# Modulation slots of the mlp_out stage: two ahead of each of its four output products, in place of four behind each of the first two

## The chip, the cores and the metric

The kernel runs on one core of a Trainium2 chip. The metric is the device time of one execution in microseconds (us). Shown with it are the span that the profiler records on that core and the TensorE clock that was granted, as a share of full speed.

## The reference, cut to what matters

The reference is a small transformer over 512 tokens of width 1024: a gMLP layer with its feed-forward part, an attention layer with its own, then a second block. A conditioning vector `c` gives each layer its shifts, scales and gates:

```
c_act = silu(c)
mod = c_act @ ada_w[layer] + ada_b[layer]            # 1024 x 6144, for two layers
sh_m, sc_m, g_m, sh_f, sc_f, g_f = split(mod, 6)
h = modulate(rms_norm(x, pre_mix_g), sh_m, sc_m)
y = gmlp_mixer(h, ...)                               # ends in (u * mixed v) @ w_out: 512x2048 @ 2048x1024
x = x + g_m * rms_norm(y, post_mix_g)
...
k, v, dcum = shared_kv(x, c_act @ kv_ada_w + kv_ada_b, ...)   # 1024 x 2048
```

The product `@ w_out` is the stage `mlp_out`. Beside it the kernel works on the products of `c_act` with the big modulation matrices. In this stage those are the two 1024-column halves of `kv_ada_w`, which are not needed before the layer behind the feed-forward part.

## The kernel before, in words

**Products.** Each matrix product is a stage of groups of 256 output columns. A group of `mlp_out` has four units of weights; a unit is four chunks of 128 rows by 256 columns (512 KB). There are four groups, called 0 to 3 here, in the code (i, j) = (0, 0), (0, 1), (1, 0), (1, 1). A unit goes through a ring of four buffers: SyncE (SP) loads `raw` (L358), ScalarE (ACT) makes `w_hi` (L702), GpSimd (POOL) makes `w_lo` in place of `raw` (L708), and TensorE (PE) takes 12 products of 256 columns for each chunk, three for each of four blocks of tokens (L1254). A buffer's next load waits on `w_used` until PE is through with the unit in it. So the first unit of a group can be loaded once the first unit of the group before has been used.

**Group 0** runs beside the token mixing: PE makes a mixed chunk (L1412), VectorE (DVE) forms `tmp` from it (L1817, L1823), ACT and POOL split it into `y_hi` and `y_lo` (L876, L1165), four chunks ahead of their use. After its last `tmp`, DVE runs `gain_copy(0)` (L1703).

**Epilogue of a group.** ACT splits all four units of the next group, then takes square sums of the finished one (L860). DVE multiplies the finished sums by a gain into `y_mlp` (`product_group`, L1725). That frees the accumulator for the group after the next.

**Modulation slots.** A slot is two chunks of 128 rows by 1024 columns of a modulation matrix (512 KB each). Slot s has the chunks 2s and 2s + 1. SP loads a chunk into one of two buffers (`ada_load`, L419) and waits before that on `ada_used`, until DVE has used the chunk two before it. DVE multiplies and adds it into `ada_wide` (`ada_chunk`, L1630 for the first chunk of eight, L1633 for the others). After four slots (eight chunks) `ada_wide` is complete; PE sums it over partitions in `wide_columns(q)` (L1305, 8 small products), and only when DVE has read that result (`wide_finish(q)`, L1646) does it start the next eight chunks. `wide_finish(q)` is called by DVE at the first chunk of the next four slots. Slots 12 to 15 make q = 3, slots 16 to 19 make q = 4, slots 20 to 23 make q = 5.

**The order on the queues in mlp_out.** SP carries its instructions out strictly in the order written: an instruction that waits holds up all loads behind it. In the kernel before it loads the eight units of groups 0 and 1; then slot 16, unit 0 of group 2, slot 17, unit 1, slot 18, unit 2, slot 19, unit 3, and in the same way slots 20 to 23 with the units of group 3. DVE runs slots 16 to 19 after the product of group 0, and slots 20 to 23 after the product of group 1. PE calls `wide_columns(3)` ahead of chunk 8 of group 0, and `wide_columns(4)` ahead of chunk 2 of group 2. `wide_columns(5)` comes with the next stage, `gu0`.

The waits behind this order are these (the first two at L418 and L356):

```
sp.wait_ge(ada_used, n + 1)     # ada_load of chunk n; ada_used starts at 2
sp.wait_ge(w_used, n + 1)       # load_unit of unit n; w_used starts at RING = 4
pe.wait_ge(ada_ready, ADA_SETUP - ADA_PAIRS + q + 1)      # wide_columns(q)
dve.wait_ge(ada_sum, ADA_SETUP - ADA_PAIRS + q + 1)       # wide_finish(q)
```

Of the kernel before, what the change touches and what calls it, by code (L numbers as in the profile page):

```python
# [120 lines left out]
def build_program(nc, io):  # L121
    S = number_stages()
    ctx = ExitStack()
    with ctx:
# [220 lines left out]
        def unit_no(st, i, j, x):  # L345
            return st.unit0 + i * st.per_body + (len(st.units[0]) if j else 0) + x

        def slot_of(st, i, j, x):

            n = unit_no(st, i if isinstance(i, int) else 0, j, x)  # L350
            return n % RING


        def load_unit(sp, st, src, i, j, x):
            n, s, (k0, nk) = unit_no(st, i, j, x), slot_of(st, i, j, x), st.units[j][x]
            sp.wait_ge(w_used, n + 1)  # L356
            for dst, ap in src(i, j, k0, nk, raw[:, s, 0:nk, :]):
                sp.dma_start(dst, ap).then_inc(landed[s], 16)  # L358
# [7 lines left out]
        src_of = {}  # L366
# [47 lines left out]
        def ada_load(sp, n):  # L414

            wide, k = 2 + n // DC, n % DC
            w, c0 = (ada_w[0], wide) if wide < 6 else (kv_ada_w, wide - 6) if wide < 8 else (ada_w[1], wide - 8)
            sp.wait_ge(ada_used, n + 1)  # L418
            sp.dma_start(ada_raw[:, n % 2, :], w[k * P:(k + 1) * P, ADA_WIDE * c0:ADA_WIDE * (c0 + 1)]).then_inc(ada_landed[n % 2], 16)  # L419

        def ada_slot_load(sp, slot):
            ada_load(sp, 2 * slot)
            ada_load(sp, 2 * slot + 1)

        def load_group(sp, name, i, j):
            st = S[name]
            for x in range(len(st.units[j])):
                load_unit(sp, st, src_of[name], i, j, x)

        def load_stage(sp, name, ada=None, unroll=False, skip=0):  # L430

            st = S[name]
            def group(i, j):
                load_group(sp, name, i, j)
                if ada:
                    ada(i, j)
            def body(i):
                group(i, 0)
                group(i, 1)
            if skip % 2:  # L440
                group(skip // 2, 1)
            first = (skip + 1) // 2
            if unroll or st.iters - first <= 1 or st.per_body % RING:

                for i in range(first, st.iters):
                    body(i)
            else:
                with sp.Fori(first, st.iters) as i:
                    body(i)
# [248 lines left out]
        def split_hi(act, st, i, j, units=slice(None)):  # L698
            for x, (_, nk) in list(enumerate(st.units[j]))[units]:
                s = slot_of(st, i, j, x)  # L700
                act.wait_ge(landed[s], landed_value(st, i, j, x))
                act.activation(w_hi[:, s, 0:nk, :], raw[:, s, 0:nk, :], ACT.Copy).then_inc(w_split_hi, 1)  # L702

        def split_lo(eng, st, i, j, units=slice(None)):
            for x, (_, nk) in list(enumerate(st.units[j]))[units]:
                s = slot_of(st, i, j, x)
                eng.wait_ge(w_split_hi, unit_no(st, i, j, x) + 1)
                eng.tensor_tensor(w_lo[:, s, 0:nk, :], raw[:, s, 0:nk, :], w_hi[:, s, 0:nk, :].bitcast(F32),  # L708
                                  ALU.subtract).then_inc(w_split, 1)
# [7 lines left out]
        def sums_tok(j):  # L717
            return acc[:, j].rearrange("p a (b n) -> p (a b) n", b=2)
# [3 lines left out]
        def _(sp):  # L722
# [31 lines left out]
            ada_slot_load(sp, 1)  # L754
            load_stage(sp, "mlp_u", lambda i, j: ada_slot_load(sp, 2 * i + j), skip=2, unroll=True)
            load_stage(sp, "mlp_v", lambda i, j: ada_slot_load(sp, 8 + 2 * i + j), unroll=True)
            load_group(sp, "mlp_out", 0, 0)
            load_group(sp, "mlp_out", 0, 1)
            st = S["mlp_out"]
            for j in range(2):  # L760
                for x in range(len(st.units[j])):
                    ada_slot_load(sp, 16 + len(st.units[0]) * j + x)
                    load_unit(sp, st, src_of["mlp_out"], 1, j, x)
            load_stage(sp, "gu0", lambda i, j: ada_slot_load(sp, 24 + 2 * i + j), unroll=True)
            load_group(sp, "down0", 0, 0)
            ada_slot_load(sp, 46)
# [481 lines left out]
        def _(pe):  # L1248
# [51 lines left out]
            def wide_columns(q):  # L1300

                pe.wait_ge(ada_ready, ADA_SETUP - ADA_PAIRS + q + 1)
                pe.wait_ge(ada_col, ADA_SETUP - ADA_PAIRS + q)
                for m in range(ADA_WIDE // P):
                    ins = pe.matmul(ada_ps[:, m:m + 1], ada_wide[:, m * P:(m + 1) * P], ones[:, 0:1], start=True, stop=True)  # L1305
                ins.then_inc(ada_sum, 1)
# [97 lines left out]
            def mix_tokens(g):  # L1404

                if g % V_PART == 0:
                    pe.wait_ge(v_norm, NB // 2 * (g // V_PART + 1))
                    pe.wait_ge(v_norm_act, NB // 2 * (g // V_PART + 1))
                if g >= 2:
                    pe.wait_ge(mix_read, g - 1)  # L1410
                for b in range(NB):
                    ins = pe.matmul(aux[:, g % 2, b * P:(b + 1) * P], v[:, b, g * P:(g + 1) * P], ws_t[:, g, :], start=True, stop=True)  # L1412
                ins.then_inc(mix_ps, 1)

            def mixing_beside(i, j, k):

                if (i, j) == (0, 0) and k + AHEAD < GC:
                    mix_tokens(k + AHEAD)
                if (i, j, k) == (0, 1, 0):
                    pe.wait_ge(gain_ready, 1)  # L1420
                if (i, j, k) in ((0, 0, 8), (1, 0, 2)):
                    wide_columns(3 + i)
            for g in range(AHEAD):
                mix_tokens(g)
# [194 lines left out]
        def _(dve):  # L1619
# [3 lines left out]
            def ada_chunk(n):  # L1623

                q, k = divmod(n, DC)
                if k == 0 and q:
                    wide_finish(q - 1)
                dve.wait_ge(ada_landed[n % 2], 16 * (n // 2 + 1))
                if k == 0:
                    dve.tensor_scalar(ada_wide[:], ada_raw[:, n % 2, :], c_act[:, 0:1], None, ALU.mult).then_inc(ada_used, 1)  # L1630
                else:
                    dve.drain()
                    dve.scalar_tensor_tensor(ada_wide[:], ada_raw[:, n % 2, :], c_act[:, k:k + 1], ada_wide[:], ALU.mult, ALU.add) \  # L1633
                        .then_inc(ada_used, 1)
                if k == DC - 1:
                    dve.drain().then_inc(ada_ready, 1)

            def ada_slot(slot):
                ada_chunk(2 * slot)
                ada_chunk(2 * slot + 1)  # L1640
# [31 lines left out]
            def modulation(gain, scale):  # L1672

                dve.scalar_tensor_tensor(scol[:], scale, 1.0, gain, ALU.add, ALU.mult)
                dve.drain()
# [25 lines left out]
            def gain_copy(n):  # L1701
                dve.wait_ge(gain_ps, n + 1)
                dve.tensor_copy(gain_row[:].rearrange("p (a t) -> p a t", a=2), sums(1)).then_inc(gain_ready, 1)  # L1703
                dve.drain()

            def add_square_sums(n, g):

                dve.wait_ge(sq_ready, 8 * n + 2 * g + 2)
                if g:
                    ins = dve.tensor_tensor(square_sum[:, 4, :], square_sum[:, 0 if g == 1 else 4, :], square_sum[:, g, :], ALU.add)  # L1710
                    if g == 3:
                        ins.then_inc(sum_ready, 1)
                    else:
                        dve.drain()

            def product_group(n, g, y):

                cols = slice(g * COLS, (g + 1) * COLS)
                for half in range(2):
                    blocks = slice(2 * half, 2 * half + 2)  # L1720
                    if half:
                        add_square_sums(n, g)
                    else:
                        dve.wait_ge(sq_ready, 8 * n + 2 * g + 1)
                    ins = dve.tensor_tensor(y[:, blocks, cols], sums_tok(g % 2)[:, blocks, :],  # L1725
                                            gain_row[:, cols].unsqueeze(1).broadcast_to([P, 2, COLS]), ALU.mult)
                ins.then_inc(acc_read["dve"], 1)
# [50 lines left out]
            for q in range(4):  # L1778
                dve.wait_ge(r_ps, q + 1)
                for n in range(4):  # L1780
                    g = 4 * q + n
# [41 lines left out]
                    dve.tensor_tensor(tmp[:, c % 4, :], tmp[:, c % 4, :], u[:, g, :], ALU.mult).then_inc(t_ready, 1)  # L1823
            gain_copy(0)
            for g in range(4):
                product_group(0, g, y_mlp)
                if g < 2:
                    for slot in range(16 + 4 * g, 20 + 4 * g):
                        ada_slot(slot)
            modulation(par_b[:, 32:40], mod[:, 32:40])  # L1830
            add_normed(0, y_mlp)
            normed("h1", scol[:], mod[:, 24:32])
# [235 lines left out]
            st = S["mix_out"]  # L2068
# [20 lines left out]
            st = S["ple"]  # L2089
# [40 lines left out]
```

## Time and profile before

| | |
|---|---|
| time, median of 3 runs | 2206.12 us (2200.85 to 2209.34) |
| the profiled execution's own time | 2205.68 us |
| its span | 2204.0 us |
| mean granted TensorE clock | 0.961 of full speed |
| busy share of the span | PE 91%, DVE 36%, ACT 35%, POOL 48% |

The span is cut by stage in the trace; `mlp_out` lies between 262 and 375 us. A row of the timeline gives start, length, engine, line, operation and the tiles written and read; the bracket tells how long the engine was idle before it and what ended that. In the chain of waits, each piece is the work or the wait that the end of the program hung on at that time. PEclk 1.00 is TensorE at its full 2.4 GHz, 0.50 is 1.2 GHz.

### The profile page before, as it was taken

The numbers are of one execution on the slowest core, as the hardware profiler recorded it, in microseconds if no ns is written. First come the engines' busy times: TensorE is split into PE (matmuls) and PEld (weight loads), VectorE is DVE, ScalarE is ACT, GpSimd is POOL, SyncE is SP. The second block draws the span as 40 slices with busy tenths as digits, with TensorE's granted clock in tenths as the row PEclk, the third lists the DMA queues.
The fourth block names the chain that finished last, engine by engine and source line by source line (L and its number), as shares of the span: only waits on it lengthen the run. The fifth ranks groups of instructions, "written<-read, shape, count | busy, mean of one in ns | idle before, by whom it ended". The sixth has DMA issues, their size and how long they took to land.

```text
span 2204.0 us, 31094 instructions
## 1 busy us (share of the span) xinstructions
PE 2006.9 (91%) x12052; PEld 1763.3 (80%) x12052; DVE 797.2 (36%) x1298; ACT 766.1 (35%) x1198; POOL 1047.3 (48%) x573
## 2 busy tenths in 40 slices
PE   5999898999998969999997999999789993988997
PEld 5889898788888958877896888899668882756897
DVE  5536754444432055263623111010357700035212
ACT  3422332433321234345634333222433321335223
POOL 2634462766763444546446555533613440615552
PEclk9999999999999989999998999999899996998999
DMA  7655354466653213222121333322212334201132
GB/s 256 214 172 163 106 163 153 137 178 184 192 153 102 87 48 88 77 86 72 53 67 58 95 95 95 95 95 88 71 48 77 96 94 78 86 29 39 50 98 84
DMA packets 238064, 232.72 MB, mean 106 GB/s; under 512 B 15016, under 2 KB 219600, under 8 KB 237696
## 3 DMA queue, kind: packets, MB, share of 16 engines
q1 hardware_dynamic: 237448, 230.97, 34.6%
q8 instruction: 83, 1.36, 0.3%
q14 instruction: 29, 0.24, 0.0%
q10 hardware_dynamic: 504, 0.15, 0.0%
HBM read 226.33 MB, written 4.75 MB: 105 GB/s over the span
## 4 chain that ended last, share of the span: by engine, by line
PE 83%; DVE 6%; DMA 4%; ACT 3%; issue 1%; DVEq 1%; SPq 1%; POOL 1%; ACTq 0%
PE acc L1254 71%; PE ms L604 2%; PE acc L579 2%; DMA raw<-in_w_in 2%; DVE x_tok L1733 1%; PE ada_ps L1305 1%; PE aux L593 1%; PE aux L1254 1%; DMA x_tok<-in_x 1%; SPq L358 1%; DMA ada_raw<-in_kv_ada_w 1%; PE aux L1450 1%; DVEq L1735 1%; DVE ada_wide L1633 0%; DVE ada_acc L1655 0%
## 5 line engine op out<-in xcount | busy, mean ns | idle before, releaser
L708 POOL TENSOR_TENSOR w_lo<-raw,w_hi 128x1024 fp32r<-128x1024 f32 (+1 forms) x300 | 742.3, 2488 | 739.8 <-ACT w_hi L702 739.4
L1254 PE MATMUL acc<-hh,w_hi 128*128 128x512 f32 x1344 | 532.8, 396 | 44.5 <-ACT ogate L991 37.4
L1254 PE MATMUL acc<-hh,w_lo 128*128 128x512 f32 x1344 | 526.6, 392 | 0.0
L1254 PE MATMUL acc<-hl,w_hi 128*128 128x512 f32 x1344 | 526.5, 392 | 0.0
L702 ACT ACTIVATE w_hi<-raw 128x1024 fp32r<-128x1024 f32 (+1 forms) x300 | 308.8, 1040 | 437.2 <-DMA raw<-in_ffn_w_down 199.1
L1254 PEld LDWEIGHTS acc<-hh,w_hi 128*128 128x128 f32 x1344 | 254.9, 190 | 107.3 <-ACT ogate L991 37.8
L1254 PEld LDWEIGHTS acc<-hl,w_hi 128*128 128x128 f32 x1344 | 254.7, 190 | 53.8 <-issue 1.7
L1254 PEld LDWEIGHTS acc<-hh,w_lo 128*128 128x128 f32 x1344 | 254.2, 189 | 54.1
L1254 PE MATMUL acc<-w_hi,hh 128*128 128x256 f32 x704 | 200.7, 285 | 0.0
L1254 PE MATMUL acc<-w_hi,act_hi 128*128 128x256 f32 x704 | 200.6, 285 | 0.0
L1254 PE MATMUL acc<-w_lo,act_hi 128*128 128x256 f32 x704 | 199.3, 283 | 0.0
L1254 PE MATMUL acc<-w_hi,hl 128*128 128x256 f32 x704 | 199.2, 283 | 0.0
L1254 PE MATMUL acc<-w_hi,act_lo 128*128 128x256 f32 x704 | 199.2, 283 | 0.0
L1254 PE MATMUL acc<-w_lo,hh 128*128 128x256 f32 x704 | 199.2, 283 | 0.0
L1633 DVE SCALAR_TENSOR_TENSOR ada_wide<-ada_raw,c_act,ada_wide 128x1024 f32<-128x1024 f32 x84 | 166.6, 1984 | 52.8 <-DMA ada_raw<-in_kv_ada_w 24.7
L1839 DVE TENSOR_TENSOR tmp<-acc,tmp 128x512 f32<-128x512 f32 x44 | 30.4, 692 | 357.6 <-ACT tmp L931 357.6
L1189 POOL TENSOR_TENSOR act_lo<-tmp,act_hi 128x512 f32 (+1 forms) x44 | 72.5, 1648 | 173.3 <-DVE act_hi L1841 173.3
L1254 PEld LDWEIGHTS acc<-w_lo,act_hi 128*128 128x128 f32 x704 | 135.3, 192 | 0.8 <-issue 0.8
L1254 PEld LDWEIGHTS acc<-w_hi,act_hi 128*128 128x128 f32 x704 | 135.3, 192 | 0.8 <-issue 0.8
L1254 PEld LDWEIGHTS acc<-w_hi,hh 128*128 128x128 f32 x704 | 135.1, 192 | 1.0 <-issue 0.5
L1254 PEld LDWEIGHTS acc<-w_lo,hh 128*128 128x128 f32 x704 | 135.1, 192 | 0.8 <-issue 0.7
L1254 PEld LDWEIGHTS acc<-w_hi,act_lo 128*128 128x128 f32 x704 | 135.2, 192 | 0.0
(370 smaller groups left out, 3053.2 us busy)
## 6 DMA issues: line engine op xcount, KB each, us to landing
raw<-in_ffn_w_gu SPq DMA_DIRECT2D x176, 256.0 KB, 3.2
ada_raw<-in_ada_w SPq DMA_DIRECT2D x80, 512.0 KB, 3.9
raw<-in_w_in SPq DMA_DIRECT2D x52, 512.0 KB, 3.6
raw<-in_ffn_w_down SPq DMA_DIRECT2D x40, 512.0 KB, 3.4
raw<-in_a_w_in SPq DMA_DIRECT2D x32, 512.0 KB, 4.9
raw<-in_a_w_out SPq DMA_DIRECT2D x16, 512.0 KB, 3.7
ada_raw<-in_kv_ada_w SPq DMA_DIRECT2D x16, 512.0 KB, 4.7
raw<-in_kv_w SPq DMA_DIRECT2D x16, 512.0 KB, 3.6
```

The lines of the kernel that those rows point to most:

```text
L358: sp.dma_start(dst, ap).then_inc(landed[s], 16)
L579: pe.matmul(bank(b)[:, 0:WIDTH[b]], a["qz"][:, e, b * P:(b + 1) * P], a["k"][:, ds(i, 1), 0:WIDTH[b]].rearrange("p a t -> p (a t)"), start ...
L593: last = pe.transpose(out[:, c:c + P], a["p"][:, e, OFF[b] + s * P:OFF[b] + (s + 1) * P], ident[:])
L604: last = pe.matmul(ms[:, b * 64:b * 64 + 64], a["pT"][:, c:c + P], a["v"][:, s, ds(h * 64, 64)], start=s == 0, stop=s == b)
L702: act.activation(w_hi[:, s, 0:nk, :], raw[:, s, 0:nk, :], ACT.Copy).then_inc(w_split_hi, 1)
L708: eng.tensor_tensor(w_lo[:, s, 0:nk, :], raw[:, s, 0:nk, :], w_hi[:, s, 0:nk, :].bitcast(F32), ALU.subtract).then_inc(w_split, 1)
L1189: pool.tensor_tensor(act_lo[:, ds(f, 1), :], tmp[:, 2 + j:3 + j, :], act_hi[:, ds(f, 1), :].bitcast(F32), ALU.subtract).then_inc(act_ready, 1)
L1254: ins = pe.matmul(out, w, x, start=first and n == 0, stop=last and n == len(pairs) - 1, skip_group_check=check)
L1305: ins = pe.matmul(ada_ps[:, m:m + 1], ada_wide[:, m * P:(m + 1) * P], ones[:, 0:1], start=True, stop=True)
L1450: pe.matmul(aux[:, t % 2, :], head_ones[:], sq[:, t % 2, :], start=True, stop=True).then_inc(hs_ps, 1)
L1633: dve.scalar_tensor_tensor(ada_wide[:], ada_raw[:, n % 2, :], c_act[:, k:k + 1], ada_wide[:], ALU.mult, ALU.add) \
L1839: dve.tensor_tensor(tmp[:, 2 + j, :], sums(j)[:, 1, :], tmp[:, j, :], ALU.mult).then_inc(acc_read["dve"], 1)
```

## The change

SP loads the slots two per group, in all four groups: one behind the second and one behind the fourth unit of each group. DVE runs two slots ahead of each product, 16 and 17 ahead of that of group 0, and so on to 22 and 23 ahead of that of group 3. PE calls `wide_columns(4)` ahead of chunk 14 of group 2, not of chunk 2.

```
-            load_group(sp, "mlp_out", 0, 0)
-            load_group(sp, "mlp_out", 0, 1)
             st = S["mlp_out"]
-            for j in range(2):
-                for x in range(len(st.units[j])):
-                    ada_slot_load(sp, 16 + len(st.units[0]) * j + x)
-                    load_unit(sp, st, src_of["mlp_out"], 1, j, x)
+            for g in range(st.groups):
+                for x in range(len(st.units[g % 2])):
+                    load_unit(sp, st, src_of["mlp_out"], g // 2, g % 2, x)
+                    if x % 2:
+                        ada_slot_load(sp, 16 + 2 * g + x // 2)
...
-                if (i, j, k) in ((0, 0, 8), (1, 0, 2)):
+                if (i, j, k) in ((0, 0, 8), (1, 0, 14)):
                     wide_columns(3 + i)
...
             for g in range(4):
+                ada_slot(16 + 2 * g)
+                ada_slot(17 + 2 * g)
                 product_group(0, g, y_mlp)
-                if g < 2:
-                    for slot in range(16 + 4 * g, 20 + 4 * g):
-                        ada_slot(slot)
```

## Rows read from the trace of the kernel before

**Rows 1.** The page: busy time of each engine, and the chain's shares by engine.

```profile
PE 2006.9 (91%) x12052; PEld 1763.3 (80%) x12052; DVE 797.2 (36%) x1298; ACT 766.1 (35%) x1198; POOL 1047.3 (48%) x573
...
PE 83%; DVE 6%; DMA 4%; ACT 3%; issue 1%; DVEq 1%; SPq 1%; POOL 1%; ACTq 0%
```

**Rows 2.** Waits, 240 to 420 us: us in total, times, longest.

```profile
PE ada_ps L1305 <- DVEq L1636: 2.4, 1, 2.4
```

**Rows 3.** The chain of waits, pieces between 270 and 375 us: start, us, what.

```profile
271.96 1.43 PE acc L1254 x12
...
318.05 5.83 DMA ada_raw<-in_kv_ada_w
...
326.71 2.61 PE ada_ps L1305 x16
329.32 45.70 PE acc L1254 x360
```

**Rows 4.** PE's timeline: wide_columns(3), first products of groups 1 and 2.

```profile
281.35 1.84 PE L1305 MATMUL ada_ps<-ones,ada_wide 128*128 128x1 f32 x16
...
298.22 0.36 PE L1254 MATMUL acc<-w_hi,y_hi 128*128 128x256 f32 x1 [0.51 <-issue]
...
321.32 0.28 PE L1254 MATMUL acc<-w_hi,y_hi 128*128 128x256 f32 x1
```

**Rows 5.** Busy time by stretch, around two pauses of PE; PEclk is the granted clock.

```profile
core 0: us, PE busy (x) PEld busy (x) DVE busy (x) ACT busy (x) POOL busy (x), PEclk, DMA share, GB/s
326.00:336.00 10.00, 9.29 (x53) 9.29 (x54) 4.74 (x7) 2.62 (x9) 2.36 (x1) 0.66 0.38 109
255.00:260.00 5.00, 4.86 (x27) 4.60 (x28) 4.76 (x9) 4.57 (x7) 0.00 (x0) 0.66 0.00 0
```

**Rows 6.** DVE's timeline: end of mixing, first chunks of slot 16, last product.

```profile
293.00 1.21 DVE L1703 COPY gain_row<-acc 128x1024 f32<-128x1024 f32 x1
...
304.79 0.15 DVE L1646 TENSOR_TENSOR mod<-ada_ps,par_a 128x8 f32<-128x8 f32 x1
304.86 0.90 DVE L1630 TENSOR_SCALAR ada_wide<-ada_raw,c_act 128x1024 f32<-128x1024 f32 x1
305.85 1.28 DVE L1633 SCALAR_TENSOR_TENSOR ada_wide<-ada_raw,c_act,ada_wide 128x1024 f32<-128x1024 f32 x1
310.38 1.89 DVE L1633 SCALAR_TENSOR_TENSOR ada_wide<-ada_raw,c_act,ada_wide 128x1024 f32<-128x1024 f32 x1 [3.24 <-DMA ada_raw<-in_kv_ada_w]
...
375.94 0.69 DVE L1725 TENSOR_TENSOR y_mlp<-acc,gain_row 128x512 f32<-128x512 f32 x1 [14.52 <-ACTq L862]
```

**Rows 7.** SP's queue: DMA issues of units (L358) and of modulation chunks (L419).

```profile
270.59 0.37 SPq L358 DMA_DIRECT2D raw<-in_a_w_out  x1
...
305.79 1.70 SPq L419 DMA_DIRECT2D ada_raw<-in_kv_ada_w  x2
```

**Rows 8.** Single unit loads, and their us from issue to landing.

```profile
L358 SPq DMA_DIRECT2D raw<-in_a_w_out x1: 368/368/368, 297.7 to 297.7; - x1
DMA to landing us min/median/max: 3.6/3.6/3.6
...
L358 SPq DMA_DIRECT2D raw<-in_a_w_in x1: 433/433/433, 223.8 to 223.8; - x1
DMA to landing us min/median/max: 5.1/5.1/5.1
...
L358 SPq DMA_DIRECT2D raw<-in_a_w_out x1: 433/433/433, 231.7 to 231.7; - x1
DMA to landing us min/median/max: 6.8/6.8/6.8
```

**Rows 9.** ACT's and POOL's timelines: a late unit split, POOL's last y chunks.

```profile
307.65 1.06 ACT L702 ACTIVATE w_hi<-raw 128x1024 fp32r<-128x1024 f32 x1 [3.52 <-DMA raw<-in_a_w_out]
...
308.79 2.39 POOL L708 TENSOR_TENSOR w_lo<-raw,w_hi 128x1024 fp32r<-128x1024 f32 x1 [3.58 <-ACT w_hi L702]
...
293.22 2.55 POOL L1165 TENSOR_TENSOR y_lo<-tmp,y_hi 128x512 fp32r<-128x512 f32 x2 [1.29 <-ACT y_hi L876]
```

## The prediction

> **What bounds the kernel now.** I read the page's busy times first: PE is busy for 91% of the span, and the chain that ended last runs over PE for 83% of it [rows 1]. So a change outside PE counts only where it makes PE wait or lets it go on. The list of waits for the stage and its surroundings, read next, has one wait inside the four groups of `mlp_out`: PE stood 2.4 us ahead of `wide_columns(4)`, for DVE's last chunk of slot 19 [rows 2]. The chain of waits shows why [rows 3]: from group 0's product on, DVE and the chunk loads take turns (a load waits for the chunk two before it; the piece at 318.05 is one such load, 5.83 us), and the 16 to 19 batch is through only at 326.7, two chunks of products after group 2 began at 321.32 [rows 4]. Everything else in groups 1 to 3 is PE alone, down to 375.0 [rows 3]. Last I read SP's queue, for the change moves its entries: in the kernel before, the first unit of group 1 is issued at 270.59, 27 us before group 1 starts at 298.22 [rows 7, 4].
>
> **What the change removes.** With slots 18 and 19 run in group 1 and `wide_columns(4)` at chunk 14 of group 2, that wait is gone. Its price has three parts. The wait is 2.4 us [rows 2]. The sums themselves took 2.61 us there, against some 1.8 at full clock in `wide_columns(3)`: 0.8 us [rows 3, 4]. And the granted clock was 0.66 over 326 to 336 us, which is 6.8 us at 1.2 GHz [rows 5]; the 30 chunks behind the wait took 45.7 us where 30 times 1.43 make 42.9 [rows 3], 2.8 us. Together 6.0 us gained.
>
> **What it adds: SP's queue behind DVE.** The number of instructions is the same (16 chunk loads, 16 chunks, 16 unit loads); only their order differs. A chunk load now stands ahead of unit loads that it can hold up. Going through the new order, the load of each slot needs DVE to have used the slot before it:
>
> - Slot 16 stands between units 1 and 2 of group 0 and needs slot 15, which DVE runs in the last group of the stage before. It hides.
> - Slot 17 stands ahead of unit 0 of group 1, and needs slot 16, which DVE now reaches only behind the whole mixing and `gain_copy(0)`. This one bites.
> - Slots 18 and 19 stand in group 1, and need slots 17 and 18. Slot 17 is run ahead of the product of group 0, so unit 2 of group 1 is issued near 303 and ready near 312, needed at 306 + 11.5 = 317.7. Slot 18 comes behind the product of group 0, which ACT allows near 311.5; unit 0 of group 2 is then issued near 316.5 and ready near 325, needed near 331.6. They hide, with 5 us to spare.
> - Slot 20 needs slot 19, used near 320. It hides.
> - Slot 21 stands ahead of unit 0 of group 3. It needs slot 20, whose first chunk on DVE calls `wide_finish(4)`, which waits for PE's `wide_columns(4)`, now at chunk 14 of 16. This bites too.
> - Slots 22 and 23 need slots 21 and 22. By the same steps unit 2 of group 3 is ready some 7 us early, and the first unit of `gu0` is issued near 376, 14 us ahead of the end of group 3. They hide. DVE runs 23 by 382, where before it idled 14.5 us ahead of the last product [rows 6].
>
> **Price of the first stall.** `gain_copy(0)` ends at 294.2 [rows 6]. From the start of the small `mod` row to the end of chunk 32 are 0.97 us, and chunk 33 takes 1.37 more with its gap [rows 6]; POOL works on its last `y_lo` until 295.77 [rows 9], and a chunk that ran beside POOL's 308.79 row took 1.89 in place of 1.28 [rows 6, 9], so I add 0.4. (This takes 0 to 1.2 us.) Chunk load 35 is thus issued at 297.0, unit 0 of group 1 at 297.4. Then it has to land. A lone load took 3.6 us; seven unit loads stand straight behind a pair of chunk loads, as here, and took 4.8 to 6.8 us, median 5.1; the lone one, the median and the longest are shown [rows 8]. I take 5.1, since the queue has the same order. ACT's start to POOL's start is 1.14 us, POOL 2.39, and 0.1 to PE's start: 3.65 us [rows 9]. PE can begin group 1 at 297.4 + 5.1 + 3.65 = 306.15, not 298.22 [rows 4]: 7.9 us.
>
> **Price of the second.** From the end of `wide_columns(4)`: 0.15 to the `mod` row, 2.37 to the second chunk load's issue, 0.4 to that of unit 0 [rows 6, 7], then 5.1 and 3.65 as above: 11.7 us. PE still has chunks 14 and 15 to do, 2.87 us [rows 3]. The stall is 8.8 us.
>
> **Price of the clock after each.** After the 2.4 us wait PE had 6.8 us at 1.2 GHz, after the pause ahead of 255 us 3.4 us (0.66 over 5 us) [rows 5]. Half of such a time is lost: 1.7 to 3.4 us for each of the two stalls. I take 2.5, the middle, as the two rows lie on both sides of these pauses: 5.0 us.
>
> [...]
>
> **Sum.** 7.9 + 8.8 + 5.0 - 6.0 = +15.7 us. The profiled execution's own time is 2205.68 us, 0.4 under the median of the runs shown, so the forecast is 2221 us, and 2222 by the median.
>
> The Trainium skill ("DMA: Bandwidth & Descriptors", Queues, rings and completion order) says that descriptors are taken in ring order but that a later transfer may complete before an earlier one. If unit 0 so landed as a lone one does, each stall would be 1.5 us shorter and the sum 3.0 lower; the seven loads behind a pair, none under 4.8 us, speak against it.
>
> **Bounds.** Landing 3.6 to 6.8 us: -3.0 to +3.4 over two stalls. Clock 1.7 to 3.4 each: -1.6 to +1.8. The DVE operations beside POOL: -0.4 to +1.2. With all on one side, +10.7 to +22.1 us: 2216 to 2228. The three runs of before lie within -5 and +3 of their median, which widens that.
>
> **Rivals.**
>
> *Only one stall bites.* If group 3's (or group 1's) first unit gets through in time, 11.3 (or 10.4) us go away and the time is 2210 or 2211. For it: each lateness is worked out from steps that were not seen in this order. Against it: the two have different causes, and the issue at 270.59 that kept group 1 safe waits in the new order for an event after 294 [rows 7, 6]. 8%.
>
> *The removed wait decides: faster.* One mechanism: PE passes chunk 2 of group 2 without its wait and keeps its full clock, and the unit loads get past the slots in time. It gives 2205.7 - 6.0 = 2200 us. It decides where the two first units are late by less than 6 us together with their clock; for the first one alone to be in time it must be issued by 298.22 - 8.75 = 289.5, and slot 16 would have to be used by 289, while DVE is at its `tmp` chunks until 293 [rows 6]. 5%.
>
> *A third stall.* The room of 5 to 7 us of unit 2 in group 3 and of unit 0 in group 2 is used up, by landings of 6.8 us and POOL slowed by DVE. One more stall of 3 us with its clock, 2.5, gives 2227; with the two at their upper bounds 2234. 8%.
>
> *It evens out within the noise* (both stalls near the lower bounds, or shorter at a place that I don't see): 2212, 4%.
>
> **How the numbers follow.** The forecast has 75%. About what a measurement of this kernel can tell from no change is 0.5%, 11 us here. Slower by more than that: the forecast but for its lowest part (70%) and the third stall (8%), 78%. Within: one stall (8%), evening out (4%), the forecast's lowest part (5%), 17%. Faster: 5%. The range is 2211 to 2231: its lower end takes in the single stall's upper value and the spread of the runs, its upper end the bounds plus 3.
>
> **What would show it.** Right: PE idle about 8 us at the start of group 1, ended by POOL's `w_lo`, and again about 9 us at the start of group 3; no idle time ahead of `wide_columns(4)`; SP issuing unit 0 of group 1 near 297 and that of group 3 about 3 us after `wide_columns(4)`; clock at 0.5 for 3 to 7 us behind each; group 3's end near 391 and all after it shifted by that, unchanged in length. Wrong: unit 0 of group 1 issued ahead of 290, or a stretch behind `mlp_out` whose length changes by over 3 us.

## The result, and the profile after

The changed kernel takes 2223.17 us (median of 4 runs, 2222.11 to 2224.21), the kernel before 2204.79 us in the same comparison (4 runs, 2200.85 to 2209.34). The ratio is 1.0077, with a 95% interval of 1.0059 to 1.0096: slower by 17 us by the ratio. The forecast was 2221 us, 15.7 over the kernel before.

The page of the changed kernel gives the engines' busy time and the chain's shares by engine, against [rows 1]:

```profile
PE 2007.2 (90%) x12052; PEld 1765.2 (79%) x12052; DVE 800.6 (36%) x1298; ACT 765.9 (34%) x1198; POOL 1048.4 (47%) x573
...
PE 83%; DVE 6%; DMA 3%; ACT 2%; issue 2%; DVEq 1%; SPq 1%; POOL 1%; ACTq 1%; PEldq 0%
```

The work is the same, 12,052 matmuls in 2007 us. What is new is waiting: the span went from 2204.0 to 2222.4 us, 18.4 more. The chain of waits through `mlp_out` tells where (start, us, what; the pieces called "issue" here are idle time of PE that the chain puts down to no releaser). One line number less than before for most lines, since the edit removed one:

```profile
296.25 1.69 PE acc L1253 x12
297.94 9.13 issue
307.06 45.60 PE acc L1253 x360
352.67 1.68 PE ada_ps L1304 x16
354.35 2.98 PE acc L1253 x24
357.32 10.21 issue
367.54 25.88 PE acc L1253 x192
```

Read against [rows 3, 4]: `wide_columns(4)` at 352.67 follows the products without a wait and takes 1.68 us, not 2.61; the old wait is gone. In its place stand two pauses, 9.1 us ahead of group 1 and 10.2 us ahead of group 3. The last piece ends at 393.4, where group 3 ended at 375.0 before. That is 18.4 us later, the whole difference of the spans, so the stages behind `mlp_out`, taken together, kept their length.

SP's queue, against [rows 7], and the landings of the two late units, against [rows 8]:

```profile
295.08 2.56 SPq L419 DMA_DIRECT2D ada_raw<-in_kv_ada_w  x2
297.69 0.98 SPq L358 DMA_DIRECT2D raw<-in_a_w_out  x2
...
355.24 1.72 SPq L419 DMA_DIRECT2D ada_raw<-in_kv_ada_w  x2
357.00 0.98 SPq L358 DMA_DIRECT2D raw<-in_a_w_out  x2
```

```profile
DMA to landing us min/median/max: 5.8/5.8/5.8
...
DMA to landing us min/median/max: 6.9/6.9/6.9
```

Group 1's first unit is issued at 297.69, 0.25 us before PE is through with group 0; before, it was issued at 270.59. The list of SP's own waits from 262 to 400 us (us in total, times, longest) names what held it:

```profile
SPq L419 <- DVE ada_wide L1629: 70.1, 2, 47.8
```

Twice SP stood for the first of eight chunks on DVE, once for 47.8 us: it got as far as slot 17 right after group 0's last unit load, and could go on only when DVE, behind all the mixing, had used chunk 32. DVE's and POOL's timelines around that chunk, against [rows 6, 9]:

```profile
292.92 1.21 DVE L1702 COPY gain_row<-acc 128x1024 f32<-128x1024 f32 x1
294.22 0.17 DVE L1645 TENSOR_TENSOR mod<-ada_ps,par_a 128x8 f32<-128x8 f32 x1
294.31 0.74 DVE L1629 TENSOR_SCALAR ada_wide<-ada_raw,c_act 128x1024 f32<-128x1024 f32 x1
295.14 2.13 DVE L1632 SCALAR_TENSOR_TENSOR ada_wide<-ada_raw,c_act,ada_wide 128x1024 f32<-128x1024 f32 x1
...
354.39 0.17 DVE L1645 TENSOR_TENSOR mod<-ada_ps,par_a 128x8 f32<-128x8 f32 x1 [14.00 <-PE ada_ps L1304]
```

```profile
293.14 3.06 POOL L1164 TENSOR_TENSOR y_lo<-tmp,y_hi 128x512 fp32r<-128x512 f32 x2 [1.29 <-ACT y_hi L875]
304.62 4.66 POOL L708 TENSOR_TENSOR w_lo<-raw,w_hi 128x1024 fp32r<-128x1024 f32 x2 [8.43 <-ACT w_hi L702]
```

The second cause is in DVE's last line: DVE sat idle 14.0 us with slot 20 before it until PE's `wide_columns(4)` let it go, and SP with all of group 3's units sat behind it. The chunk beside POOL's `y_lo` took 2.13 us in place of 1.28, and the two `y_lo` 3.06 in place of 2.55.

Last, the clock around and behind the pauses:

```profile
core 0: us, PE busy (x) PEld busy (x) DVE busy (x) ACT busy (x) POOL busy (x), PEclk, DMA share, GB/s
298.00:307.00 9.00, 0.00 (x0) 0.00 (x0) 2.57 (x2) 2.11 (x2) 2.38 (x2) 0.71 0.94 304
307.00:317.00 10.00, 9.94 (x65) 9.97 (x66) 4.34 (x4) 3.68 (x10) 7.03 (x3) 0.75 0.29 98
357.00:367.00 10.00, 0.32 (x3) 0.12 (x1) 2.57 (x2) 2.11 (x2) 1.91 (x1) 0.64 0.93 303
367.00:377.00 10.00, 9.46 (x57) 9.50 (x58) 3.87 (x4) 3.89 (x11) 7.48 (x4) 0.68 0.29 102
```

The granted clock is below 1.00 already within each pause (0.71 and 0.64). PEclk 0.75 over 10 us is 5.0 us at 1.2 GHz behind the first pause, 0.68 is 6.4 us behind the second. The DMA engines are 93 to 94% busy in the pauses: the loads that SP had held back all run at once.

### The profile page after: what moved, and what is told of

Its sections match the earlier page's. It is cut to its first block, busy times and chain, and to the rows that moved or that the text cites. A ratio compares the mean times of both kernels' runs of the same rounds, so it can differ in the third digit from the quotient of the medians.

```text
span 2222.4 us, 31094 instructions
## 1 busy us (share of the span) xinstructions
PE 2007.2 (90%) x12052; PEld 1765.2 (79%) x12052; DVE 800.6 (36%) x1298; ACT 765.9 (34%) x1198; POOL 1048.4 (47%) x573
## 4 chain that ended last, share of the span: by engine, by line
PE 83%; DVE 6%; DMA 3%; ACT 2%; issue 2%; DVEq 1%; SPq 1%; POOL 1%; ACTq 1%; PEldq 0%
PE acc L1253 71%; PE ms L604 2%; PE acc L579 2%; DMA raw<-in_w_in 2%; DVE x_tok L1732 1%; PE ada_ps L1304 1%; PE aux L593 1%; PE aux L1253 1%; SPq L358 1%; DMA x_tok<-in_x 1%; PE aux L1449 1%; DVEq L1734 1%; DVE tmp L1948 1%; DVE score L1936 1%; PE aux L1411 0%
```

## The experiments

Two theories. **Q**: unit loads stand behind slot loads on SP, and these wait for DVE. **D**, the rival: chunks on DVE ahead of the products delay the epilogues and slow POOL. All runs give the ratio to the kernel before on the same chip, with its 95% interval.

| run | what differs | ratio | interval | group 3 ends at |
|---|---|---|---|---|
| before | | 1 | | 375.0 |
| changed | | 1.0077 | 1.0059 to 1.0096 | 393.4 |
| e1_sp_order | changed, SP's order mended at both places | 0.9976 | 0.9960 to 0.9992 | 370.8 |
| e2_after_k2 | changed, `wide_columns(4)` at chunk 2 | 1.0019 | 1.0006 to 1.0033 | 379.8 |
| e3_sp_first | changed, SP's order mended at group 1 | 1.0027 | 1.0012 to 1.0042 | 381.8 |
| e4_before_k8 | before, `wide_columns(4)` at chunk 8 | 0.9972 | 0.9955 to 0.9988 | 369.4 |
| e5_after_k8 | changed, `wide_columns(4)` at chunk 8 | 1.0036 | 1.0022 to 1.0050 | 384.4 |
| e6_before_k14 | before, `wide_columns(4)` at chunk 14 | 1.0005 | 0.9992 to 1.0018 | 374.1 |
| e7_filler | changed, pauses filled with products | 1.0060 | 1.0042 to 1.0077 | 389.0 |
| e8_after_again | changed, once more | 1.0080 | 1.0063 to 1.0098 | 393.0 |
| e9_unit1_later | changed, no unit load right behind the first | 1.0082 | 1.0060 to 1.0105 | 393.0 (391.9) |
| e10_unit0_between | changed, first unit between two chunk loads | 1.0068 | 1.0044 to 1.0091 | 389.7 (388.6) |

In the profiled executions of the last two, group 0 itself ran 1.1 us later than in the others; the value in brackets has that taken off.

**SP's order alone, at both places.** DVE and PE run exactly as in the changed kernel.

```
+            behind = {(0, 1): (16,), (1, 2): (17,), (1, 3): (18, 19),
+                      (2, 1): (20,), (3, 2): (21,), (3, 3): (22, 23)}   # (group, unit): slots loaded behind it
             for g in range(st.groups):
                 for x in range(len(st.units[g % 2])):
                     load_unit(sp, st, src_of["mlp_out"], g // 2, g % 2, x)
-                    if x % 2:
-                        ada_slot_load(sp, 16 + 2 * g + x // 2)
+                    for slot in behind.get((g, x), ()):
+                        ada_slot_load(sp, slot)
```

> The changed kernel with SP's queue alone reordered: the first three units of group 1 are loaded ahead of slot 17, and the first three of group 3 ahead of slot 21; DVE and PE as in the changed kernel. Theory Q (the loss is unit loads standing behind slot loads on SP): both PE pauses of 9 and 10 us vanish with their slow clock, the 2.4 us wait ahead of wide_columns(4) stays gone, so 6 us under the kernel before: 2199 us, ratio 0.997. Rival D (the loss comes from running chunks on DVE ahead of the products, which delays the epilogues and slows POOL): the DVE order is the same, so the time stays at 2223, ratio 1.008.

It measured 2202.24 us against 2207.36 for the kernel before beside it, ratio 0.9976 (expected 0.997). The chain of waits of this kernel:

```profile
297.96 1.65 issue
299.61 43.43 PE acc L1254 x360
343.04 1.68 PE ada_ps L1305 x16
344.72 26.03 PE acc L1254 x216
```

The second pause is gone and of the first 1.65 us are left. D falls as the cause of the loss: DVE's order is untouched, and the time went from the changed kernel's 1.0077 to below the kernel before. A small part of D holds. Group 1 starts at 299.61 here and at 298.22 in the kernel before, behind 0.51 us [rows 4], so 1.4 us are left. They are POOL's, whose `y_lo` and `w_lo` ran beside DVE's early chunks:

```profile
293.14 3.06 POOL L1165 TENSOR_TENSOR y_lo<-tmp,y_hi 128x512 fp32r<-128x512 f32 x2 [1.29 <-ACT y_hi L876]
296.17 12.39 POOL L708 TENSOR_TENSOR w_lo<-raw,w_hi 128x1024 fp32r<-128x1024 f32 x4
```

Four `w_lo` take 12.39 us here; in the kernel before they took 9.47, beginning at 295.73. The first of them is what group 1 waits for. Group 3 ends 4.2 us earlier than in the kernel before, the 5.6 gained by the missing wait less these 1.4. That DVE's chunks are what slows POOL is read from their running side by side; no run takes the chunks away at this place alone.

**`wide_columns(4)` back at chunk 2.**

```
-                if (i, j, k) in ((0, 0, 8), (1, 0, 14)):
+                if (i, j, k) in ((0, 0, 8), (1, 0, 2)):
```

> The changed kernel with wide_columns(4) back at chunk 2 of group 2. Theory Q: slot 20 can start 17 us earlier, so slot 21 no longer holds up group 3's first unit. The second pause (10.2 us and 2.9 us of clock) goes, the first (8.8 and 2.5) stays, and PE finds the 16 to 19 batch ready at chunk 2: 2223 - 13 = 2210 us, ratio 1.0025. Rival D: the place of wide_columns(4) changes nothing in DVE's order ahead of the products, 2223 us. A third view, that moving wide_columns(4) to chunk 14 is what removed the old 2.4 us wait: then that wait comes back here and the time is some 2216.

Measured 1.0019 against the 1.0025 of theory Q. Its chain:

```profile
298.04 8.87 issue
306.91 27.94 PE acc L1253 x216
334.85 1.68 PE ada_ps L1304 x16
336.53 43.31 PE acc L1253 x360
```

The first pause stands, the second is gone, and there is no wait at chunk 2. So the earlier slots on DVE are enough to remove the old wait, and the move to chunk 14 isn't needed for it. (The move alone removes it too, as two runs below show.) What the move brought is the second pause. The first pause and its clock, less the 6 us gained, make this run's +0.2%.

**SP's order at group 1 alone** (slot 17 behind three units of group 1; slot 21 stays ahead of group 3's first).

```
+            behind = {(0, 1): (16,), (1, 2): (17,), (1, 3): (18, 19),
+                      (2, 1): (20,), (2, 3): (21,), (3, 1): (22,), (3, 3): (23,)}
```

> The changed kernel with SP's queue reordered at group 1 alone (three units ahead of slot 17, slot 18 and 19 behind the fourth); group 3's first unit still stands behind slot 21. Theory Q: the first pause (8.8 us and 2.5 us of clock) goes and the second stays: 2223 - 11 = 2212 us, ratio 1.0033. Rival D: 2223.

Measured 1.0027 against 1.0033: the mirror image of the run before. In its chain the first pause is 1.65 us and the second stands:

```profile
297.96 1.65 issue
...
347.69 9.37 issue
```

**The kernel before, with `wide_columns(4)` at chunk 8.** One number of the kernel before is changed.

```
-                if (i, j, k) in ((0, 0, 8), (1, 0, 2)):
+                if (i, j, k) in ((0, 0, 8), (1, 0, 8)):
```

> The kernel before with wide_columns(4) at chunk 8 of group 2 in place of chunk 2, nothing else. If the old wait was worth 6.0 us (2.4 waiting, 0.8 in the sums, 2.8 in the products at the lower clock), it gives 2205 - 6 = 2199 us, ratio 0.9973: the 16 to 19 batch is ready at 326.6 and chunk 8 comes near 333. Group 3's fourth unit is then ready only 1.6 us ahead of its use. If the wait costs its idle time alone, 2202.5. If it was hidden, 2205.

Measured 2201.06 us against 2207.36 for the kernel before beside it, ratio 0.9972 (expected 0.9973). In its trace 326 to 336 us are at full clock, against 0.66 in [rows 5]:

```profile
326.00:336.00 10.00, 10.00 (x86) 10.00 (x86) 4.57 (x7) 3.69 (x10) 3.22 (x2) 1.00 0.56 166
```

Group 3 ends at 369.4, 5.6 us earlier than before. So the gain that was forecast as 6.0 us was real, and a move by six chunks collects it with no edit elsewhere.

**A smaller dose of the second cause.** The changed kernel with chunk 8.

```
-                if (i, j, k) in ((0, 0, 8), (1, 0, 14)):
+                if (i, j, k) in ((0, 0, 8), (1, 0, 8)):
```

> The changed kernel with wide_columns(4) at chunk 8 of group 2 (chunk 14 in the changed kernel, chunk 2 in the run before this). A dose of the second cause. In the changed kernel group 3's first unit was ready 13.2 us behind the end of wide_columns(4); PE now has 8 chunks, 11.5 us, to do in that time in place of 2.9. Theory Q: second pause 1.7 us (1 to 2.5) in place of 10.2, and a clock loss of 0 to 3.4 us behind it; with the first pause 2213 us (2212 to 2216), ratio 1.003. If the second pause had another cause than that queue, it stays and the time is 2223.

Measured 1.0036; expected 1.003. The second pause is 2.1 us at chunk 8 (1.7 expected), 10.2 at chunk 14, none at chunk 2:

```profile
344.27 1.68 PE ada_ps L1304 x16
345.95 11.62 PE acc L1253 x96
357.57 2.14 issue
359.70 24.74 PE acc L1253 x192
```

Even behind 2.1 us the 192 products took 24.74 us, where group 1 in the kernel before took 23.1 [rows 4]: the clock's price, 1.6 us, is almost as large as the pause's.

**The PE part of the change alone**, `wide_columns(4)` at chunk 14 in the kernel before.

```
-                if (i, j, k) in ((0, 0, 8), (1, 0, 2)):
+                if (i, j, k) in ((0, 0, 8), (1, 0, 14)):
```

> The kernel before with wide_columns(4) at chunk 14 of group 2, nothing else: the PE part of the change alone. The old wait goes (-6.0 us). SP's old order has group 3's first unit ahead of slot 21, but its second unit behind it: ready some 13.2 us behind the end of wide_columns(4), needed 2.9 + 5.7 = 8.6 us behind it. Theory Q: a pause of 4.6 us (3 to 6) at the second unit of group 3, with 1.7 to 3.4 us of clock: +7, together +1, so 2207 us, ratio 1.0005 (0.999 to 1.002). If the place of wide_columns(4) costs nothing by itself, 2199.

Measured 1.0005, as expected; the gain of 6 us is eaten up. The pause is now inside group 3, at its second unit, and POOL's `w_lo` ends it: 3.2 us of PE waiting (4.6 expected, 3 to 6), behind a load that the chain shows from its issue at 345.63.

```profile
342.99 2.64 PE acc L1254 x22
345.63 5.76 DMA raw<-in_a_w_out
...
354.95 13.13 PE acc L1254 x96
```

The profiled execution took 2202.55 us, at the low end of its 12 runs (2202.09 to 2215.77). So the verdict rests on the ratio; the trace shows only where the pause is.

**The clock's share.** The pauses are filled with products into a bank that the stage doesn't use.

```
+            def filler(i, j):
+                if j == 0:
+                    for _ in range(70 + 8 * i):
+                        pe.matmul(ms[:, 0:COLS], y_hi[:, 0, 0:P], y_hi[:, 0, 0:COLS], start=True, stop=True)
-            gemm("mlp_out", y_hi, y_lo, h_ready, CH["y"], unroll=True, before_chunk=mixing_beside)
+            gemm("mlp_out", y_hi, y_lo, h_ready, CH["y"], filler, unroll=True, before_chunk=mixing_beside)
```

> The changed kernel with idle PE time filled: behind groups 0 and 2 PE runs 70 and 78 products of 256 columns into an unused bank (8.4 and 9.3 us at full clock), inside the pauses of 9.1 and 10.2 us. The pauses keep their length; only what PE does in them changes. If the products behind a pause are slow because of the pause's idle time (5.4 us of the loss by the trace), the clock stays at 2.4 GHz and the time falls by 5.4, to 2218 us, ratio 1.005. If the clock's price is not due to the idle time, 2223.

> The changed kernel as it is, as the reference of this job's others on the same chip: ratio 1.0077 as in the first measurement (1.006 to 1.0095), 2223 us.

Measured 2220.49 us, and 2224.69 for the changed kernel beside it: 4.2 us less for doing 148 useless products, where 5.4 were expected (ratios 1.0060 and 1.0080; the two intervals overlap, so the time alone shows it weakly). The trace shows it plainly. The stretch behind each filled pause is at full clock, and the 360 products take 43.43 us, against 44.81 in the execution of the changed kernel profiled beside it (45.60 in the first). Group 3 ends 4.0 us earlier than in that execution, 3.4 of them by faster products:

```profile
307.00:317.00 10.00, 9.76 (x81) 9.79 (x82) 3.66 (x4) 3.69 (x10) 7.26 (x4) 1.00 0.32 112
365.00:375.00 10.00, 9.27 (x77) 9.30 (x78) 2.92 (x3) 3.90 (x11) 7.76 (x4) 1.00 0.33 111
```

**The landing of the late units.** Two runs asked why they landed in 5.8 and 6.9 us, where 5.1 was forecast. In the first no unit load is issued right behind the first one (slots 18 and 22 stand between, and their loads follow 2.6 and 3.5 us behind it). Chunk loads by number, behind (group, unit):

```
+            behind = {(0, 1): (32, 33), (0, 3): (34, 35), (1, 0): (36, 37), (1, 3): (38, 39),
+                      (2, 1): (40, 41), (2, 3): (42, 43), (3, 0): (44, 45), (3, 3): (46, 47)}
```

> The changed kernel with slot 18 ahead of the second unit of group 1 and slot 22 ahead of the second unit of group 3, so that no other unit load is issued right behind the first one. In the changed kernel the late first units landed 5.8 and 6.9 us after their issue, where the prediction had 5.1. If the load behind it (0.5 us later) shares the DMA engines with it and makes the difference, they land in 5.1 (4.8 to 6.0) here, the two pauses shrink by 0.7 and 1.8 us: 2221 us, ratio 1.0068. If the two chunk loads ahead make it, the landings stay at 5.8 and 6.9, and the time at 2223.

The landings stayed at 5.9 and 6.6 us, and the ratio at 1.0082. The unit load right behind is not the reason.

In the second the first unit stands between the two chunk loads, with one load ahead of it and one behind:

```
+            behind = {(0, 1): (32, 33), (0, 3): (34,), (1, 0): (35,), (1, 1): (36, 37), (1, 3): (38, 39),
+                      (2, 1): (40, 41), (2, 3): (42,), (3, 0): (43,), (3, 1): (44, 45), (3, 3): (46, 47)}
```

> The changed kernel with the first unit of groups 1 and 3 between the two chunk loads of slots 17 and 21, so that it waits for one chunk on DVE and not two, and has one load ahead of it. Theory Q: issued near 295.5 and 355.6 in place of 297.7 and 357.0, landing in 4.5 us (3.9 to 5.1): pauses shorter by 3.5 and 3.8 us, the clock's price as before or 1 us less: 2216 us, ratio 1.0045 (1.003 to 1.0055). Rival D (the DVE order): 2223, ratio 1.008.

```profile
299.08 6.51 issue
...
356.23 7.96 issue
```

The pauses shrank by 2.6 and 2.2 us, less than the 3.5 and 3.8 expected, for the landings took 5.4 and 6.1 us with only one load ahead, where 4.5 was expected. The measured ratio, 1.0068 (1.0044 to 1.0091, 5 runs over 12 us), can't tell this from the changed kernel; by its trace group 3 ends 4.8 us earlier (4.4 against the second execution of the changed kernel). By time it is inconclusive.

A third candidate is in the traces already: how far apart the two chunk loads ahead are issued. Shown are two pairs of the changed kernel with a unit load straight behind them, and slot 21 in e1_sp_order, which stands ahead of group 3's fourth unit there. A length of 3.7 us means that the second load is issued 3.3 us after the first, one of 1.72 that it is issued 1.4 us after it:

```profile
229.17 3.75 SPq L419 DMA_DIRECT2D ada_raw<-in_ada_w  x2
...
240.60 1.72 SPq L419 DMA_DIRECT2D ada_raw<-in_kv_ada_w  x2
```

```profile
345.61 3.69 SPq L419 DMA_DIRECT2D ada_raw<-in_kv_ada_w  x2
```

The units behind them landed in 5.3, 6.5 and 5.1 us. A chunk load landed 3.6 to 3.8 us after its issue here, so behind a pair 3.3 us apart only one load is still on its way, and behind one 1.4 us apart both are. Over the twelve profiled executions, the `a_w_in` and `a_w_out` loads straight behind a pair whose first load landed within 4.6 us took 5.2 us in the median with the pair some 3.3 us apart (4.4 to 7.2, 75 loads) and 6.6 with 1.4 us (5.7 to 7.5, 35 loads). Group 1's late unit, behind a pair 2.2 us apart, took 5.5 to 6.3 in six executions. The spacing goes with the landing, though the ranges overlap; no run set it by itself, so it is argued and not shown.

**A version that beats both kernels** came out twice: the changed kernel with SP's order mended (0.9976) and the kernel before with `wide_columns(4)` at chunk 8 (0.9972). Their intervals overlap widely; the second is the smaller edit.

## Why the prediction was right

The measured time lies in the range of 2211 to 2231 us, 2 us off the forecast. Point by point, in the order of its sum:

- **The removed wait, 6.0 us.** Right: its kernel alone gave 5.6 us by the trace and 0.28% by the ratio. The 30 chunks behind the wait take 43.4 us at full speed, not the 42.9 of the sum, and the small sums 1.68, not 1.8: 2.4 + 0.9 + 2.3.
- **Slot 17 ahead of group 1's first unit, 7.9 us.** Right in place and cause. PE began group 1 at 307.06, not 298.22: 8.8 us. The unit was issued at 297.69 (forecast 297.4) and landed in 5.8 us (forecast 5.1).
- **Slot 21 ahead of group 3's first unit, 8.8 us.** Right in place and cause, too small: 10.2 us. Issued 2.65 us behind the end of `wide_columns(4)` (forecast 2.9), landed in 6.9 us (forecast 5.1). This landing is the term that was mis-sized. The 5.1 is the median of seven unit loads behind a pair of chunk loads; in five of the seven that pair was issued 3.3 us apart. The one whose pair was issued as close as slot 21's (1.4 us) and that stood straight behind it is the 6.8 of [rows 8], which the sum had as its upper bound; with it the stall is 10.5. (An eighth load behind a pair, at 66.8 us, took 6.6 and isn't among the seven.) In this place and order the load took 6.0 to 7.5 us in the seven executions that were profiled with it, and never landed as a lone one does. That the spacing is the reason is argued above and not shown.
- **The clock, 5.0 us.** Right as a cause, the exact hit in part luck: the 360 products took 45.60 us where the two mended orders show 43.42 at full speed, the last 192 took 25.88 where 23.1 are full speed, 2.2 and 2.8, together 5.0 us. The 5.0 and 6.4 us at 1.2 GHz lie between the two rows that bounded them [rows 5]. In the second profiled execution of the same kernel the two terms are 1.4 and 2.2, together 3.6, behind pauses 0.5 and 0.4 us longer. With the pauses filled the loss all but went away.
- **What was said to hide** hid: group 2 began without a pause, no slot held a unit in group 2, and the span's end moved by no more than group 3's did.
- **The sum.** 8.8 + 2.2 + 10.2 + 2.8 - 5.6 = 18.4 us, as in the spans, against 15.7 forecast. Of the 2.7 between them 2.3 are the pauses, by their landings, and 0.4 the wait removed.

On the rivals: only one stall, tried by mending the other, gave 1.0019 and 1.0027, so both are needed for the whole loss. The faster outcome is what the change gives once SP's queue is out of the way. What was not foreseen is that POOL alone would have started group 1 1.4 us late, which the first pause covered: its `y_lo` and `w_lo` ran slower beside DVE's early chunks. In the bounds, the upper value of DVE's operations beside POOL should be +0.8, since 0.4 of the 1.2 is in the sum already; the upper end is +21.7 and not +22.1, and nothing hangs on it.

## What to carry to other kernels

Work moved on one engine moves waits into the in-order queue that feeds it: go through that queue entry by entry, and ask of each entry that waits what stands behind it and when that is needed. A prefetch that depends on late work belongs behind the loads that don't depend on it. A wait of TensorE can cost more than twice its length (2.4 us of waiting cost 5.6 here), for the products behind it run at the lower clock; its price is read from the granted clock behind the nearest pauses. The time that a load takes is read from loads with the same loads ahead of them, at the same distance.

## What the runs showed of the hardware that was not expected

- A pause of 2.1 us was followed by 1.6 us of clock loss. The pauses of 6.5 to 10.6 us were followed by 1.4 to 2.8, without order by length: in two executions of the changed kernel 9.1 us by 2.2 and 10.2 by 2.8, then 9.6 by 1.4 and 10.6 by 2.2. Products without use in the pause kept the granted clock at 1.00.
- A 512 KB load landed in 3.6 us alone. Straight behind a pair of its size it took 5.2 us in the median when the pair was issued 3.3 us apart (4.4 to 7.2) and 6.6 when it was 1.4 us apart (5.7 to 7.5). A unit load issued 0.5 us behind it added nothing that could be seen (5.9 and 6.6 us without it, 5.8 and 6.9 with it). With one load ahead in place of two it took 5.4 and 6.1 us; with two, 5.5 to 6.3 and 6.0 to 7.5 over all executions.
- DVE's chunk of 128x1024 took 1.28 us alone and 2.13 beside POOL's subtraction, and POOL's four `w_lo` took 12.39 us in place of 9.47 beside DVE's chunks: both engines took longer when they met.
